# Ranking of the next unit's keys on VectorE in steps zero to four instead of one to five

## The reference

```python
q = (x @ w_q).reshape(B, S, PEER_HEADS, 2, PEER_HALF)
scores = jnp.einsum('bshpk,hpnk->bshpn', q, sub_keys)
s1, i1 = lax.top_k(scores[:, :, :, 0, :], PEER_TOPK)      # 16 of 128
s2, i2 = lax.top_k(scores[:, :, :, 1, :], PEER_TOPK)
cand = (s1[..., :, None] + s2[..., None, :]).reshape(B, S, PEER_HEADS, PEER_TOPK * PEER_TOPK)
top_s, top_c = lax.top_k(cand, PEER_TOPK)                 # 16 of 256
ids = take(i1, top_c // 16) * 128 + take(i2, top_c % 16)
gates = jax.nn.softmax(top_s, axis=-1)
...
h = jnp.einsum('thkd,td->thk', jnp.take(u_tab, idb, axis=0), xb)
act = gb * jax.nn.gelu(h, approximate=False)
out = jnp.einsum('thk,thkd->td', act, jnp.take(v_tab, idb, axis=0))
```

## Time and profile before

| | us |
|---|---|
| median of 3 runs | 1428.06 |
| the profiled execution | 1427.62 |
| its span, first to last instruction | 1425.9 |
| TensorE busy | 1128.2 |
| VectorE busy | 1078.4 |
| ScalarE busy | 937.3 |
| GpSimd busy | 571.7 |

### The profile page before, as it was taken

One profiled execution on the slowest core, in us unless ns is written; L12 is line 12 of the kernel. 1 busy time (PEld: TensorE's weight loads), 2 busy tenths in 40 slices (PEclk: granted clock), 3 DMA queues, 4 the chain that ended last, 5 costly groups with the idle time before them and its releaser, 6 DMA issues.

```text
span 1425.9 us, 19360 instructions
## 1 busy us (share of the span) xinstructions
PE 1128.2 (79%) x6804; PEld 883.7 (62%) x6804; DVE 1078.4 (76%) x2602; ACT 937.3 (66%) x1613; POOL 571.7 (40%) x535
## 2 busy tenths in 40 slices
PE   9999999988689877696757888778568766767657
PEld 4567777677677677575646556666466656546545
DVE  1488776778878787688757668977888788878768
ACT  2246677669888888766636666657666766667563
POOL 1044444334544444444424434444444443434342
PEclk9999999999889989999759988998868987887988
DMA  9799999999999999999999999999999999999994
GB/s 345 284 381 426 420 425 390 427 422 426 423 426 402 425 422 427 426 426 419 427 428 426 426 425 423 419 406 426 426 427 427 426 426 425 420 424 419 426 426 163
DMA packets 89787, 584.06 MB, mean 410 GB/s; under 512 B 9709, under 2 KB 15253, under 8 KB 22490
## 3 DMA queue, kind: packets, MB, share of 16 engines
q0 software_dynamic: 74288, 536.90, 90.0%
q1 hardware_dynamic: 15402, 45.92, 8.2%
HBM read 580.69 MB, written 2.10 MB: 409 GB/s over the span
## 4 chain that ended last, share of the span: by engine, by line
DMA 47%; PE 21%; DVE 17%; issue 7%; ACT 5%; POOL 2%; POOLq 0%; SPq 0%; DVEq 0%; ACTq 0%
DMA arena<-in_uv,ids 47%; DVE arena L1819 9%; PE ps L1187 7%; PE ps L1006 2%; PE ps L872 2%; ACT arena L1445 2%; POOL arena L658 2%; PE ps L702 1%; PE ps L692 1%; PE ps L1082 1%; PE ps L685 1%; ACT actv L1438 1%; PE ps L766 1%; PE ps L769 1%; PE ps L949 0%
## 5 line engine op out<-in xcount | busy, mean ns | idle before, releaser
L658 POOL DMA_INDIRECT arena<-in_uv,ids x512 | 558.2, 1090 | 791.7 <-DVE hid L1819 539.4
L1187 PE MATMUL ps<-ident,arena 128*128 128x128 f32 x4076 | 612.1, 310 | 280.8 <-ACT arena L1445 279.8
L1187 PEld LDWEIGHTS ps<-ident,arena 128*128 128x128 f32 x4076 | 536.8, 160 | 378.5 <-ACT arena L1445 339.7
L1819 DVE CUSTOM_DVE_ANT_1 arena<-arena 128x1024 f32<-128x1024 f32 x384 | 468.2, 1224 | 194.9 <-DMA arena<-in_uv,ids 191.8
L1445 ACT ACTIVATE arena<-arena,actv 128x1024 f32<-128x1024 f32 x511 | 554.2, 1131 | 0.2
L1435 ACT ACTIVATE gel<-hid 128x2 f32<-128x2 f32 (+1 forms) x257 | 52.0, 203 | 369.8 <-DVE hid L1819 369.3
L1819 DVE CUSTOM_DVE_ANT_0 arena<-arena 128x1024 f32<-128x1024 f32 x128 | 155.6, 1225 | 63.8 <-DMA arena<-in_uv,ids 62.9
L1438 ACT ACTIVATE actv<-gel,gates 128x1 f32<-128x1 f32 x511 | 122.9, 287 | 8.4
L872 PE MATMUL ps<-arena 128*128 128x128 f32 x992 | 118.8, 279 | 0.0
L872 PEld LDWEIGHTS ps<-arena 128*128 128x128 f32 x992 | 116.7, 197 | 0.0
L1006 PE MATMUL ps<-arena 128*128 128x384 f32 x192 | 65.9, 486 | 0.0
(11 more groups left out here) (268 smaller groups left out, 1004.9 us busy)
## 6 DMA issues: line engine op xcount, KB each, us to landing
arena<-in_wq SPq DMA_DIRECT2D x10, 1024.0 KB, 9.2
arena<-in_uv,ids POOLq DMA_INDIRECT x519, 10.3
arena<-in_w_out SPq DMA_DIRECT2D x2, 2048.0 KB, 12.0
arena<-in_w_gate SPq DMA_DIRECT2D x1, 4096.0 KB, 16.8
arena<-in_w_out SPq DMA_DIRECT2D x3, 1024.0 KB, 13.1
arena<-in_w_k SPq DMA_DIRECT2D x4, 512.0 KB, 8.5
arena<-in_w_q SPq DMA_DIRECT2D x2, 1024.0 KB, 10.2
arena<-in_w_v SPq DMA_DIRECT2D x2, 1024.0 KB, 10.9
```

What stands on the lines that cost most here:

```text
L658: nc.gpsimd.indirect_dma_start(out=row(u, c)[:, 0:n], out_offset=None, in_=a["uv"][:, :], in_offset=bass.IndirectOffsetOnAxis(ap=ids[:, u ...
L1187: i = mm(ps[:, run_bank(r) + k // 4, (k % 4) * P:(k % 4 + 1) * P], row(u, c)[:, D + k * P:D + (k + 1) * P], ident[:, :], is_transpose=True ...
L1819: v.tensor_tensor_reduce(out=r, in0=r, in1=x1[t], scale=1.0, scalar=0.0, op0=ALU.mult, op1=ALU.add, accum_out=hid[:, i, c:c + 1]).then_inc ...
```

## The change

In the loop on VectorE the pieces come one step earlier for all units but unit 1. The first piece of unit u + 2 stands in step 7 of unit u, after its two dots and ahead of the background of that step; the second piece of unit u + 1 stands in step 0, and the other three in steps 1 to 3. For u = 0 the ranking of unit 1 stays in steps 2 to 5. No function changes and no other engine.

```diff
                     if u and RUN[u] != RUN[u - 1] and g == (0 if RUN[u] < 3 else 1 if RUN_END[RUN[u - 1]] in (21, 26) else 5):
                         add_run(RUN[u - 1])
+                    if u == 0 and g in (2, 3):
+                        rank_keys(1, g - 2)
+                    if g == 7 and u + 2 < NU:
+                        rank_keys(u + 2, 0)
+                    if u and g == 0 and u + 1 < NU:
+                        rank_keys(u + 1, 1)
                     if u + 1 < NU:
-                        first = 0 if u else 2
-                        if g in (first, first + 1):
-                            rank_keys(u + 1, g - first)
-                        if g == (first + 2 if u else 3):
+                        if g == (1 if u else 3):
                             rank_sums(u + 1)
-                        if g == (first + 3 if u else 4):
+                        if g == (2 if u else 4):
                             rank_rest(u + 1)
-                        if g == (first + 4 if u else 5):
+                        if g == (3 if u else 5):
                             rank_ids(u + 1)
```

## The result

The changed kernel takes 1441.07 us (median of 6 runs, 1438.73 to 1445.07), the kernel before beside it 1429.15 us (6 runs, 1426.65 to 1432.38). The ratio is 1.009 (95% interval 1.0073 to 1.0108): 11.9 us slower by the medians. Forecast were 1439 us and a chance of 0.80 for slower. In the step numbers of this text the ranking of a unit now stands in step 7 of the unit two ahead of it and in steps 0 to 3 of the one after that, where it stood in steps 0 to 4.

What follows compares the result with a forecast made beforehand. The 16 DMA engines were taken as the bound, from first gather to last. Boundary losses 4.2 + 3.0 + 1.7 + 0.3 + 3.1 - 1.0 = 11.3 us on 1427.6 gave 1438.9, forecast as 1439 us, range 1428 to 1450.

Steps and rivals of the forecast that it cites:

- 7.9 us for a dry queue: Gather time from issue to landing once the DMA queue is empty; against the usual 10.4 us it leaves 2.5 to spare.
- Item 2: In step 7 VectorE waits for TensorE's key scores, holding up the next dots; some 33 us in all at 20 boundaries.
- Units 0 to 1: At this boundary a 2.5 us wait plus 1.71 us, with no VectorE idle time to absorb it: loss 4.2 us.
- Eight others: Eight boundaries where other VectorE work stands at step 7 or 0: 0.3 to 1.3 us each, together 3.1.
- Units 23 to 24: At this boundary a 1.8 us wait plus 1.71 us, less 1.8 the gather has over: loss 1.7 us.
- Item 3: Later pieces come one step earlier; the last is 0.55 us longer than the first, so delay grows up to that by step 3.
- Units 2 to 4: Boundaries 1 to 2, 2 to 3, 3 to 4: gathers held by TensorE anyway, loss 0.3 us together, an estimate.
- Item 4: Step 4 loses its piece, returning 2.26 us to VectorE per unit; lost DMA time stays lost; -1.0 us given back overall.
- A: Rival: the ring of gathered rows absorbs every delay, no change, 1428 us (1426 to 1430); chance 0.14.
- B: Rival: faster, as the emptied step 4 returns DMA dips, 1424 us; chance 0.06.
- C: Rival: the delay feeds on itself through late ScalarE, TensorE and next scores, 1455 us; chance 0.08.
- D: Rival inside the forecast: scores cannot come before row 12, so the first half runs after the wait, not a step earlier.

Runs made afterwards that it cites:

- probe: The kernel before with unused VectorE work added in step 7 of units 11, 15, 16 and 20 (2.2, 6.5, 5.0, 3.6 us): 1429.42 us, one run.
- first_only: The kernel before with the change for unit 2 alone, all other units ranked as before: 1433.18 us in one run, against a median of 1428.89.
- keys_only: The kernel before with only the first half of the keys moved to step 7, the other four pieces left in place: 1436.18 against 1429.61 us.
- wait_only: The kernel before with VectorE also waiting in step 7 for the scores of unit u + 2, no work moved: 1434.31 against 1429.61 us.
- rest_only: The kernel before with both halves of the keys in step 0, later pieces in steps 1 to 3, nothing in step 7: 1437.89 us, ratio 1.0048.
- after_bg: The changed kernel with the first half behind the background of step 7 instead of ahead of it: 1433.04 against 1429.61 us for the kernel before.
- keys_after_bg: The kernel before with only the first half of the keys moved to step 7, behind that step's background: 1431.03 against 1428.52 us.
- keys_of_9: The kernel before with only unit 9's first half moved, into step 7 of unit 7: 1428.10 against 1428.89 us, ratio 0.999.

## Why the prediction was right, point by point

- **The bound** (every VectorE delay is to be asked if it runs the DMA queue dry): right. Share and rate fall in the units where it was said, VectorE's busy time is unchanged, and probe makes the same dip by itself, 1.01 to 0.91.
- **7.9 us for a dry queue, 2.5 us of slack**: right in size. Probe gives 2.6. The Trainium skill's price ("DMA: Bandwidth & Descriptors", section "Anatomy of one DMA — SWDGE (gpsimd) path"), by which 6.0 us are to spare, would have hidden all of probe's pieces; one cost 2.7 us. This case's traces don't agree with it here: the shortest of before's gathers took 5.7 us.
- **Item 1, the first half costs 1.71 us and is mostly covered**: right. 0.5 us over its control where there is no wait; 1.71 to the digit in unit 1.
- **Item 2, the wait**: right. 33 us at 20 boundaries were read from before; it is 32.9 at 21. After unit 1 it is 3.81. That reading needs no model: the end of TensorE's scores against the end of the dot, in one timeline. That the totals agree to 0.1 us is in part luck: after unit 2 it is 4.19 where 2.8 was read, after unit 6 1.08 for 2.8, after unit 18 there is none for 1.8.
- **Units 0 to 1**: 4.2 forecast, 4.0 in after, 5.1 in first_only. **Units 5 to 6**: 3.0, and 3.1. **Eight others**: 3.1, and 4.7.
- **Units 23 to 24**: 1.7, and 2.9; undersized. The sum took the queue there to have 1.8 us over the earlier trace rows. In after the wait is 2.63 us where 1.8 was read. The timeline of after:

```profile
1098.81 1.23 DVE L1819 CUSTOM_DVE_ANT_1 arena<-arena 128x1024 f32<-128x1024 f32 x1 [1.43 <-DMA arena<-in_uv,ids]
...
1102.04 0.61 PE L884 MATMUL ps<-arena,qs 128*128 128x128 f32 x4
...
1102.68 0.30 DVE L1649 MAX8 top<-ps 128x8 f32<-128x128 f32 x1 [2.63 <-PE ps L884]
...
1106.62 1.23 DVE L1819 CUSTOM_DVE_ANT_1 arena<-arena 128x1024 f32<-128x1024 f32 x1
...
1108.12 1.68 POOL L658 DMA_INDIRECT arena<-in_uv,ids  x1 [4.21 <-DVE hid L1819]
```

  That explains 0.8 of the 1.2 us. keys_only lost 2.7 us in this unit, wait_only 2.0 and rest_only, without the wait, 2.0: either cause alone costs something here. The sum also left out here the 0.55 us of item 3, which it has in units 0 to 1 and 5 to 6.
- **Units 2 to 4**: 0.3 forecast, 2.8 in after. In keys_only they give back 1.1, in rest_only 0.8, in after_bg they cost 2.1. The estimate "held by TensorE anyway" was too low for after; how much of the 2.8 belongs to that one execution stays open.
- **Item 3, the later pieces** ("grows by up to 0.55 us by step 3"): this is the part that failed. Its figure is right to the digit in unit 1 (3.68 in step 0, 4.23 in step 4), but it priced only how much longer a piece is than the one before it. What it left out is where a delay is paid back: if the later pieces stay, step 0 is free, and 1.71 us come back at once (2.15 left, in keys_only). By moving them the change keeps VectorE 1.7 to 2.3 us behind for four steps more (read in unit 1). That cost 5.3 us on top of keys_only, and the later pieces, with both halves in step 0, cost 8.3 us (1.0048) with next to no wait. The sum could come out right because it let the delay last to step 3, as it does in the changed kernel; but it put all of it down to the wait and the first half, and so keys_only was expected at 9 to 12 us and came at 6.6.
- **The total**, 11.3 for 11.9: partly luck. The terms above add up to more in the trace of after than forecast (units 24, 2 to 4 and the eight others are 5.3 us over together), and that trace holds some 5.5 us of the two executions' own; which terms these belong to can't be told.
- **Item 4 and "given back", -1.0**: inside unit 8 of after the landings go from 10.9 to 9.9 us behind, but the unit as a whole loses 0.7. Unit 8 as a whole gives back 2.0 us in keys_only and 1.7 in keys_after_bg, where step 0 is the one without a piece, not step 4.
- **Item 5**, ids and scores sooner, priced at nothing: no wait speaks against it.
- **What the changed profile would show**: share under 0.95 was said for three windows. It is 0.91 in the first, 0.98 in 345 to 375, and 0.95 in 1100 to 1120, which is where unit 24 begins in after; in the window as named, 1090 to 1100, it is 1.01. So one of three held as written. Rows 5 to 9 of unit 1 land 1.7 to 3.1 us later than before, not about 4; 3.3 is reached by its end. The rates tell more: 343 for 417 GB/s over 20 us is 3.5 us lost, 375 for 428 is 2.5, and 398 for 425 over 30 us is 1.9 of the 3.1 that unit 6 lost.
- **The rivals.** A, absorbed: true of twenty boundaries (2.4 us together), not of the kernel. B: seen inside one unit (1.4 to 2.0 us), not in the time of any kernel. C: not seen. D, inside the forecast: as said.

**Open:** what part of the 17.6 us of landing shift in the trace of after is that execution's own, by unit; the exact share of the two causes, and if they add; what of the wait's price is paid through late background in place of late dots; and if keys_of_9 is faster than before. No kernel here beats before by more than its interval.

## What to carry to other kernels

Before work is moved ahead in an in-order engine, read at each place when its input ends against when the engine would get there; the difference is the new wait, and everything queued behind pays it. Then ask at which later step the engine has less to do than before, for a delay lasts until there: here moving the whole chain of pieces sooner kept it alive for four steps more, and moving one piece alone paid that piece's own time back in the next step. If the piece must go early, try it behind other work of the same step. If its input is to be made sooner instead, measure that alone as a control: here it opened waits in other queues and lost 12.1 us.

## What the runs showed of the chip that was not expected

- DMA engines at a share of 1.01 still took a delay of the engine for which their issuer waits: 3.6 us of added VectorE work in a calm unit cost 0.5 us or nothing, 6.5 us cost 2.7 (a single run).
- Where the kernel's VectorE was busy for 25.6 of 27 us, a delay of about 4.2 us in one place cost 4 to 5 us, and it stayed in the landings up to the end, 1200 us later (4.3 after unit 30 in first_only).
- after and after_bg differ in the place of one piece of 1.71 us within a step, VectorE being busy for 1077.1 and 1076.3 us, and their times are 1441.07 and 1433.04 us: the order within one step of one engine is worth 8 us.
